# Placing weight tiles and moving tiles in SBUF: distances modulo 256 bytes, phase by phase

## What is computed

```python
for l in range(2):        # first block, 272 tokens
    h = h + 0.5 * swiglu(rmsnorm(h), w_gate, w_up, w_down)      # 1024 -> 2816 -> 1024
    h = h + hybrid_mixer(rmsnorm(h), ...)                       # stick-breaking attention + conv
    h = h + 0.5 * swiglu(rmsnorm(h), ...)
h = rmsnorm(h)[:, 16:]
for i in range(2):        # second block, 256 tokens
    x = x + 0.5 * swiglu(rms(x), ...)
    h = x + mixer_i(rms(x))                                     # 0: differential attention, 1: retention
    x = h + 0.5 * swiglu(rms(h), ...)
```

## Time and profile before

| | |
|---|---|
| median of 3 runs | 2210.6 us (2204.15 to 2211.57) |
| profiled execution | 2210.91 us, its span 2209.1 us |
| TensorE busy | 2198.0 us, 18114 matmuls |
| VectorE busy | 1602.4 us |
| ScalarE busy | 1276.6 us |
| GpSimd busy | 282.1 us |
| HBM read | 384.18 MB, 174 GB/s over the span |

### The profile page before, as it was taken

The page is one execution under the profiler, slowest core; times in us unless marked ns, Lnnn a source line. Parts: engine busy times, 40 slices in busy tenths (PEclk is TensorE's granted clock), DMA queues, the critical chain, the costliest instruction groups (busy, mean ns, idle before and its releaser), DMA issues.

```text
span 2209.1 us, 48942 instructions
## 1 busy us (share of the span) xinstructions
PE 2198.0 (99%) x18114; PEld 2180.8 (99%) x18114; DVE 1602.4 (73%) x2450; ACT 1276.6 (58%) x1988; POOL 282.1 (13%) x328
## 2 busy tenths in 40 slices
PE   8999999999999999999999999999999999999999
PEld 8999999999999999999999999999999999999999
DVE  6655997665566579887768767888768766777775
ACT  6444786544444368766546646876556645565662
POOL 0001661100100136220020012010010010101000
PEclk9999999999999999999999999999999999999999
DMA  6555435555455544455555555355556645445553
GB/s 229 174 188 165 159 122 170 167 171 195 155 173 183 179 161 144 144 185 186 190 169 193 195 183 163 124 178 194 195 181 200 219 162 177 161 162 194 188 200 124
DMA packets 100408, 386.68 MB, mean 175 GB/s; under 512 B 11312, under 2 KB 12464, under 8 KB 100304
## 3 DMA queue, kind: packets, MB, share of 16 engines
q1 hardware_dynamic: 99648, 383.89, 52.2%
q0 software_dynamic: 368, 1.26, 0.2%
q10 hardware_dynamic: 288, 0.12, 0.0%
HBM read 384.18 MB, written 1.05 MB: 174 GB/s over the span
## 4 chain that ended last, share of the span: by engine, by line
PE 98%; ACT 1%; DVE 1%; issue 0%; DMA 0%; ACTq 0%
PE bank L387 16%; PE bank L389 15%; PE bank L388 15%; PE bank L395 15%; PE bank L396 14%; PE bank L397 14%; PE bank L759 1%; PE bank L1049 1%; PE bank L1050 1%; PE bank L1051 1%; PE bank L1096 0%; PE bank L709 0%; PE bank L740 0%; PE bank L940 0%; PE bank L943 0%; PE bank L942 0%
## 5 line engine op out<-in xcount | busy, mean ns | idle before, releaser
L412 DVE TENSOR_TENSOR wlo<-raw,whi 128x1024 fp32r<-128x1024 f32 (+1 forms) x677 | 893.3, 1322 | 177.8 <-ACT whi L405 165.4
L405 ACT ACTIVATE whi<-raw 128x1024 fp32r<-128x1024 f32 (+1 forms) x677 | 745.5, 1112 | 164.5 <-PE bank L389 117.2
L387 PE MATMUL bank<-u,whi 128*128 128x272 f32 (+1 forms) x1888 | 549.0, 291 | 7.1 <-DVE u L450 7.1
L389 PE MATMUL bank<-u,wlo 128*128 128x272 f32 (+1 forms) x1888 | 543.7, 288 | 0.0
L388 PE MATMUL bank<-u,whi 128*128 128x272 f32 (+1 forms) x1888 | 541.9, 287 | 0.0
L395 PE MATMUL bank<-u,whi 128*128 128x256 f32 x1888 | 529.2, 280 | 0.2
L397 PE MATMUL bank<-u,wlo 128*128 128x256 f32 x1888 | 527.4, 279 | 0.0
L396 PE MATMUL bank<-u,whi 128*128 128x256 f32 x1888 | 527.4, 279 | 0.0
L387 PEld LDWEIGHTS bank<-u,whi 128*128 128x128 f32 x1888 | 356.9, 189 | 8.0 <-DVE wlo L412 7.3
L388 PEld LDWEIGHTS bank<-u,whi 128*128 128x128 f32 x1888 | 357.0, 189 | 0.9 <-issue 0.2
L397 PEld LDWEIGHTS bank<-u,wlo 128*128 128x128 f32 x1888 | 357.6, 189 | 0.0
(11 more groups left out here) (332 smaller groups left out, 3448.8 us busy)
## 6 DMA issues: line engine op xcount, KB each, us to landing
raw<-w SPq DMA_DIRECT2D x552, 512.0 KB, 3.4
raw<-w SPq DMA_DIRECT2D x128, 704.0 KB, 4.1
h<-xT SPq DMA_DIRECT2D x4, 272.0 KB, 4.9
outT<-h SPq DMA_DIRECT2D x8, 128.0 KB, 4.7
consts<-cst POOLq DMA_DIRECT2D x1, 576.0 KB, 4.6
dist<-cst POOLq DMA_DIRECT2D x1, 192.0 KB, 2.7
rdist<-cst POOLq DMA_DIRECT2D x1, 192.0 KB, 3.0
sgain<-small POOLq DMA_DIRECT2D x1, 145.5 KB, 4.8
```

The source lines that it names most:

```text
L387: pe.matmul(out, w_h, x_hi, start=first, stop=False)
L389: return pe.matmul(out, w_l, x_hi, start=False, stop=last)
L405: act.activation(whi[:, n % RING, 0:COLS[n]], raw[:, n % RING, 0:COLS[n]], ACT.Copy).then_inc(hi_ready, 1)
L412: dve.tensor_tensor(wlo[:, n % RING, 0:COLS[n]], raw[:, n % RING, 0:COLS[n]], whi[:, n % RING, 0:COLS[n]], ALU.subtract).then_inc(lo_ready, 1)
```

## The change

It adds a gap of 16 elements behind each weight tile of a K8 panel in the phases up to 4 (`GAP_STEP` = 144 elements from tile to tile, in `whi` and `wlo` but not in `raw`), a step of 320 instead of 272 elements between the tiles of hid at 272 tokens (`HID_STEP`), and for each phase a place of the high half and a further shift of the low half of u and of hid (`U_PLACE`, `HID_PLACE`). u grows by 104 elements a partition; `RY_PAD` shrinks by the same number. All products and their order stay.

```diff
-U_PAD, HID_PAD, RY_PAD = 112, 24, 144
+RY_PAD, GAP_STEP, HID_STEP = 40, 144, 320
+U_PLACE = {0: (48, 0), 1: (48, 32), 2: (32, 16), 3: (48, 48), 4: (32, 0), 5: (48, 48), 6: (48, 16), 8: (48, 0), 9: (48, 32), 10: (32, 16), 11: (48, 0), 12: (0, 48), 7: (48, 16)}
+HID_PLACE = {0: (32, 0), 2: (48, 32), 3: (48, 48), 5: (16, 32), 7: (32, 48), 9: (16, 16), 10: (32, 32), 12: (0, 32)}
...
-        u = sb("u", [128, 2 * KD * T], f32r)
+        u = sb("u", [128, 2 * KD * T + 104], f32r)
...
-            hid = sb("hid", [128, 2 * FT * T], f32r, area)
+            hid = sb("hid", [128, 2 * FT * HID_STEP + 96], f32r, area)
...
-        def tile_of(buf, tiles, pad, y, part, k, c0, c1):
-
-            width, first, at = (T, 0, 0) if y <= LAST_MIX else (SEQ, META, pad)
-            at += part * tiles * width
-            parts = buf[:, at:at + tiles * width].rearrange("p (k c) -> p k c", c=width)
+        def tile_of(buf, tiles, step, place, y, part, k, c0, c1):
+
+            first = first_col(y)
+            at = part * tiles * step + sum(place[:part + 1])
+            parts = buf[:, at:at + tiles * step].rearrange("p (k c) -> p k c", c=step)
             return parts[:, k, c0 - first:c1 - first]
 
         def u_at(y, part, k, c0=None, c1=T):
-            return tile_of(u, KD, U_PAD, y, part, k, first_col(y) if c0 is None else c0, c1)
+            return tile_of(u, KD, width(y), U_PLACE[y], y, part, k, first_col(y) if c0 is None else c0, c1)
 
         def hid_at(y, part, f):
-            return tile_of(hid, FT, HID_PAD, y, part, f, first_col(y), T)
+            return tile_of(hid, FT, HID_STEP if y <= LAST_MIX else SEQ, HID_PLACE[y], y, part, f, first_col(y), T)
...
-        def products(pe, out, slot, k, x_hi, x_lo, first, last):
-
-
-            w_h, w_l = whi[:, slot, k * 128:k * 128 + 128], wlo[:, slot, k * 128:k * 128 + 128]
+        def weights(w, n):
+
+            tiles, step = COLS[n] // 128, GAP_STEP if n < BASE[LAST_MIX + 1]["P"] and COLS[n] == K8 else 128
+            return w[:, n % RING, 0:tiles * step].rearrange("p (k c) -> p k c", c=step)[:, :, 0:128]
+
+        def products(pe, out, n, k, x_hi, x_lo, first, last):
+
+
+            w_h, w_l = weights(whi, n)[:, k, :], weights(wlo, n)[:, k, :]
...
-                act.activation(whi[:, n % RING, 0:COLS[n]], raw[:, n % RING, 0:COLS[n]],
+                act.activation(weights(whi, n), raw[:, n % RING, 0:COLS[n]].rearrange("p (k c) -> p k c", c=128),
                                ACT.Copy).then_inc(hi_ready, 1)
...
-                dve.tensor_tensor(wlo[:, n % RING, 0:COLS[n]], raw[:, n % RING, 0:COLS[n]],
-                                  whi[:, n % RING, 0:COLS[n]], ALU.subtract).then_inc(lo_ready, 1)
+                dve.tensor_tensor(weights(wlo, n), raw[:, n % RING, 0:COLS[n]].rearrange("p (k c) -> p k c", c=128),
+                                  weights(whi, n), ALU.subtract).then_inc(lo_ready, 1)
```

More of the change, by code:

```diff
@@ L389, in products, with split_products @@
             return pe.matmul(out, w_l, x_hi, start=False, stop=last)
-        def split_products(pe, out, slot, k, x_hi, x_lo, first, last):
-            w_h, w_l = whi[:, slot, k * 128:k * 128 + 128], wlo[:, slot, k * 128:k * 128 + 128]
+        def split_products(pe, out, n, k, x_hi, x_lo, first, last):
+            w_h, w_l = weights(whi, n)[:, k, :], weights(wlo, n)[:, k, :]
             pe.matmul(out[:, 0:SEQ], w_h, x_hi, start=first, stop=False, skip_group_check=True)
@@ L632, in gate_up @@
                             if N == SEQ:
-                                mm = split_products(pe, bank[g % 4], n % RING, k, u_at(uy, 0, k),
+                                mm = split_products(pe, bank[g % 4], n, k, u_at(uy, 0, k),
                                                  u_at(uy, 1, k), k == 0, k == KD - 1)
                             else:
-                                mm = products(pe, bank[g % 4][:, 0:N], n % RING, k, u_at(uy, 0, k),
+                                mm = products(pe, bank[g % 4][:, 0:N], n, k, u_at(uy, 0, k),
                                               u_at(uy, 1, k), k == 0, k == KD - 1)
@@ L664, in tile @@
                             if both:
-                                mm = split_products(pe, bank[4 + j % 2], n % RING, k, x(0, K), x(1, K), K == 0, K == last)
+                                mm = split_products(pe, bank[4 + j % 2], n, k, x(0, K), x(1, K), K == 0, K == last)
                             else:
-                                mm = products(pe, bank[4 + j % 2][:, 0:N], n % RING, k, x(0, K), x(1, K),
+                                mm = products(pe, bank[4 + j % 2][:, 0:N], n, k, x(0, K), x(1, K),
                                               K == 0, K == last)
@@ L690, in in_panel @@
                             pe.wait_ge(u_ready, u_base(y) + (KD - 2 if k == 0 else k + 1))
-                        mm = products(pe, bank[j % MIX_BANKS][:, 0:cols], (P + j) % RING, k, u_at(y, 0, k, T - cols),
+                        mm = products(pe, bank[j % MIX_BANKS][:, 0:cols], P + j, k, u_at(y, 0, k, T - cols),
                                       u_at(y, 1, k, T - cols), k == 0, k == KD - 1)
@@ L810, in mix @@
                                               (ao_hi[:, k, W2], ao_lo[:, k, W2]))[part]
-                                mm = products(pe, bank[g % MIX_BANKS][:, 0:N2], n % RING, 4 * ff + k, x_hi,
+                                mm = products(pe, bank[g % MIX_BANKS][:, 0:N2], n, 4 * ff + k, x_hi,
                                               x_lo, k == 0, k == 3)
@@ L816, in out_tile @@
                     for k in range(k0, k1):
-                        mm = products(pe, bank[MIX_OUT[f]][:, 0:N2], (P + 44 + f) % RING, k, qk[:, k, W2], qk[:, KD + k, W2],
+                        mm = products(pe, bank[MIX_OUT[f]][:, 0:N2], P + 44 + f, k, qk[:, k, W2], qk[:, KD + k, W2],
                                       k == 0, k == KD - 1)
@@ L851, in in_panel2 @@
                     if PHASES[y] == "rt" and acc < 4 * RT_HEADS:
-                        mm = split_products(pe, bank[panel_bank(acc)], (b["P"] + j) % RING, k, u_at(y, 0, k), u_at(y, 1, k),
+                        mm = split_products(pe, bank[panel_bank(acc)], b["P"] + j, k, u_at(y, 0, k), u_at(y, 1, k),
                                              k == 0, k == KD - 1)
                         continue
-                    mm = products(pe, bank[panel_bank(acc)][:, 0:SEQ], (b["P"] + j) % RING, k, u_at(y, 0, k, META),
+                    mm = products(pe, bank[panel_bank(acc)][:, 0:SEQ], b["P"] + j, k, u_at(y, 0, k, META),
                                   u_at(y, 1, k, META), k == 0, k == KD - 1)
```

## The result

The changed kernel takes 2224.6 us (median of 4 executions, 2223.8 to 2226.0) where the kernel before, beside it, takes 2210.8 (2204.2 to 2211.6): a ratio of 1.007, with a 95% interval of 1.005 to 1.009. It is slower by 0.7%, where I had forecast 2.3% faster. The profiled execution has a span of 2224.2 us against 2209.1.

The account below looks back on a forecast made before the run. TensorE, which nothing starves, bounds the kernel through the start-to-start distance of some 18,100 matmuls. 2210.9 - 30.4 - 8.4 + 2 - 14.1 = 2160.0 us, range 2142 to 2212.

Parts of the forecast that it names:

- (a): 1024-column panels up to phase 4 (u, qk, ao): gaps fix the distance, 4896 matmuls reach 120.0 ns, -30.4 us.
- (b): hid at 272 tokens: step 320 fixes the distance, 1584 matmuls reach 120.0 ns, -8.4 us.
- (c): 256-token phases: new distances per phase and half; four of five feed-forwards fast instead of two, -14.1 us.
- the floor: Least start-to-start distance of matmuls: 113.3 ns at 256 tokens, estimated 120.0 ns at 272.
- the 2 us given back: Mixers (phases 1 and 4): attention matmuls between panels depend on DVE and ACT; 2 us added to the forecast.
- The prediction's own sign: A steady stage between the levels 113.3 and 117.8 ns would make the two-level sum fail; above 117.8, R4 true.
- four of nine: Fixed-distance stretches counted at the floor: five feed-forwards, two phase 8 panels, dy with dw, ry; grounds for (a).
- (d) to (f): Phases 8 and 11 within 1 us; splits cost nil; loads and splits keep up in feed-forwards, mixers lose 2 us.
- R4: Slower: costlier rhythm in phases 0 to 4, +4.5 us; feed-forwards 9 and 10 lose theirs, +14.1; 2229.5; chance 0.15.
- its first test: R4 decided by more than 126.2 ns a matmul over u in the first three feed-forwards.
- R3: All stages: the distance modulo 256 isn't what matters; time stays at 2211 us; chance 0.12.
- R1: Everything reaches the floor, at 272 and 256 tokens, 67.8 us less: 2143.1 us; chance 0.15.

Follow-up runs that it names:

- the fastest version: Changed kernel with distance 192 in phases 0 to 4 and 112 in 256-token feed-forwards, u of phases 8 and 11, and ry: 2175.4 us, ratio 0.984.
- The kernel with equal halves: Changed kernel with high and low half at the same distance, another distance by phase: 2228.6 us in a single execution.
- pad112: Kernel before with U_PAD 28 and HID_PAD 4, moving u and hid of all 256-token phases from distance 192 to 112: 2188.4 us, ratio 0.989.
- undo256: Changed kernel with every 256-token place of u and hid back at distance 192, both halves alike: median 2208.9 us, ratio 1.001.
- entry2: Kernel before with a further 2-column matmul in front of the norm's in each 256-token feed-forward: median 2204.4 us, ratio 0.998.

## Why the prediction was wrong, step by step

**What bounds the kernel: right.** TensorE waits for about 8 us in the trace of after (and for 9 in that of the fastest version), and the time is the sum of the distances between starts.

**The step that failed** is one, used in (a), (b) and (c): that a fixed distance, whichever it is, has two levels only, the floor and 4.45 ns above it. The runs show a pace by distance instead, 113.2 to 120.0 ns at 256 tokens and 123.2 to 127.1 at 272. Of the 65 us between forecast and result, 33 are in phases 0 to 4 (-36.8 forecast with the 2 us given back, about -4 measured) and some 34 in the 256-token feed-forwards (-14.1 forecast, about +20 measured); the other phases take a little off. The prediction's own sign for it came: steady stages between and above the levels, 118.7, 119.2 and 121.1 ns.

**(a), the gaps, -30.4 us: nearly all of it missing.** I took the floor of 120.0 ns for fixed distances at 272 tokens because "four of nine" fixed stretches were at their floor. That census was of two distances only, 192 and once 64; it said nothing on others, and nothing on 272 columns. Measured, u goes from 126.2 to 124.2, 125.1 and 126.2, a gain of some 4 us over phases 0 to 4. The bound I had for a costlier rhythm, a whole 16-cycle step (126.7), is where hid of feed-forward 0 is now, and u at 224 went past it later (127.1).

**(b), hid, -8.4 us:** 126.5, 124.2 and 124.2 against 125.3; nothing within 0.3 us. The same step.

**(c), the places, -14.1 us: wrong in sign.** Measured about +20 us (7.0, 11.9 and 1.6). My two-level picture, 113.3 or 117.8 for any place, holds for distance 192. The trace of before had no row of another fixed distance at 256 tokens but dy with dw, and I read that row as "64 reaches the floor". The kernel with equal halves has 64 in four stretches, all at 117.6 to 117.8. dy with dw comes right behind dy at 192 in its fast rhythm; in the changed kernel, where dy is at 96, the same pair at the same 64 is slow as well. With all distances equal that pair is slow in pad112 and fast in shift160. So that row showed an inherited rhythm, not a price. What unequal halves cost by themselves stays open; 121.1 ns at 128 with 192 is above what either distance showed alone.

**(d) to (f): right in the main.** Phase 8 moved by +0.8 and phase 11 by -1.5 us, where I had less than 1, the splits cost nothing (1321 and 1112 ns against 1322 and 1112), and at 113.3 ns in all five feed-forwards no wait comes back. The 2 us that I gave back in the mixers for waits were not there: in the changed kernel the waits behind the first are 0.2 us each.

**The spread of the runs: half right.** I took 7.4 us for one feed-forward that changes its rhythm; undo256 and entry2 show it on four and three steps. But I took it as a detail that fitted, where it said that the time of the kernel before is itself drawn from levels, so that a distance without a slow draw was the thing to look for.

**The rivals.** R4 came nearest, 2229.5 against 2224.6, with its second half: feed-forwards 9 and 10 lose their pace. That the numbers lie so near is in part luck: its first half, +4.5 us in phases 0 to 4, was about -4, and feed-forward 10 lost more than its pace. Its place and its first test were wrong: u in the first three feed-forwards never went above 126.2. The other sign, a stage above 117.8, is what came. R3, that the distance doesn't matter, falls with pad112: two constants, 1.1%. The price list by distance is what R1 and my forecast both lacked.

"TensorE: Matmul & The Clock Gate" (Part 2) and "SBUF — State Buffer" (Who interferes with whom) of the Trainium skill have it that the loading of weights takes no read bandwidth from a running matmul and that TensorE waits for nobody. By that rule pad112, equal work at other distances, would have stayed at 2211; it took 2188.4. The measurement decides: that the placement can't matter, as I had read out of the rule, doesn't hold here. Whether it is the loading of weights that the moving tile meets, no run tells.

**What stays open.** Why 112 is free and 96 and 128 are not; why 192 has two rhythms and what draws them; what 160 and 208 do from one execution to the next; what unequal halves cost; what part the step from weight tile to weight tile has at 272 tokens. No run looks inside the memory, so I name no mechanism, only that at 256 tokens the distance between the weight tiles and the moving tiles modulo 256 bytes sets the price, together with the rhythm in which the stream was entered.

## What to carry to other kernels

Where TensorE never waits and its clock is full, divide the time by the number of matmuls, stage by stage: two values for one shape are a finding worth a search, and the search is cheap, since one kernel can hold another distance in each stage. Repeat the stages that matter: a single execution doesn't show whether a place has a second pace. Give the candidates a step of 16 bytes, not 64, and prefer a place that gives the same pace in each execution to one whose best draw is as good. And do not price a placement by rows of another placement: a fast stretch may have inherited its pace from the one in front.

## What was not expected of the hardware

- With 256 columns in fp32r the distance from start to start depends on where the moving tile lies relative to the weight tiles modulo 256 bytes: with equal halves from 113.2 ns (112) to 120.0 ns (0, 80), 6% at full clock, in steps of 16 bytes with no order to be seen; with 128 and 192 for the halves it was 121.1.
- One distance, 192, has two paces, 113.3 and 117.8 ns; the choice differs from execution to execution, holds for a whole feed-forward of some 180 us, and changes where matmuls of another shape stand in the stream (seen in entry2). The times of the kernel before stand on steps of 7 us, one feed-forward's worth. Two more places showed both paces: 192 with 0 for the halves (119.2 and 117.8) and dy with dw at 64 (113.2 and 117.6).
- Shifting everything by 160 bytes doesn't change the time: 2188.5 against 2188.4 us.
- With 272 columns no placement tried got below 123.2 ns (hid at 112 wasn't better than at 192), where the pace of 256 columns and 16 columns more would make 120.0. There one distance has another pace over u than over hid (64: 125.1 and 126.6).
